# Ten instead of nine slots for the expert weights, in loops over five items

## What is computed

```
logits = xt @ w_router + b_router            # 256 x 32
top_vals, top_idx = top_k(logits, 4); gates = softmax(top_vals)
for each expert e, for its tokens xb:
    hgu  = xb @ w_up_gate[e] + b_up_gate[e]  # 1024 -> 2048
    glu  = minimum(hgu[:, :1024], 7); lin = clip(hgu[:, 1024:], -7, 7)
    hact = glu * sigmoid(1.702 * glu) * (lin + 1)
    y    = hact @ w_down[e] + b_down[e]      # 1024 -> 1024
    out[tokens] += gate * y
```

## Time and profile before

| | |
|---|---|
| time, median of 3 runs | 1927.2 us (1921.48 to 1930.23) |
| profiled execution, span from first to last instruction | 1927.9 us |
| TensorE busy | 1778.7 us (92%) |
| VectorE, ScalarE, GpSimd busy | 765.1, 494.2, 195.9 us |
| moved by the DMA queues | 554.21 MB, mean 287 GB/s |
| expert stage, from SyncE's first issue to TensorE's first work of the next stage | 167.8 to 1106.2 us |
| mean granted clock of TensorE | 0.979 of full speed |

### The profile page before, as it was taken

The page is one execution under the profiler, slowest core; times in us unless marked ns, Lnnn a source line. Parts: engine busy times, 40 slices in busy tenths (PEclk is TensorE's granted clock), DMA queues, the critical chain, the costliest instruction groups (busy, mean ns, idle before and its releaser), DMA issues. The chain is left out here.

```text
span 1927.9 us, 28825 instructions
## 1 busy us (share of the span) xinstructions
PE 1778.7 (92%) x11622; PEld 1109.2 (58%) x11622; DVE 765.1 (40%) x1324; ACT 494.2 (26%) x792; POOL 195.9 (10%) x141
## 2 busy tenths in 40 slices
PE   7998999999998998999988889999999999999997
PEld 6764333333333333333333368978998778858996
DVE  8844211111111011011111186946554764456554
ACT  4623100000000000000000145444442333224442
POOL 4620000000000000000000055430000104200000
PEclk8998999999999999999999999999999999999999
DMA  7365999999999999999999946564531532145530
GB/s 284 137 245 226 398 430 429 429 430 429 430 430 430 430 430 430 430 429 430 430 429 430 381 153 234 186 228 177 200 146 24 200 109 89 64 157 196 201 127 33
DMA packets 104725, 554.21 MB, mean 287 GB/s; under 512 B 17441, under 2 KB 27682, under 8 KB 79218
## 3 DMA queue, kind: packets, MB, share of 16 engines
q1 hardware_dynamic: 104370, 553.25, 70.7%
q10 hardware_dynamic: 288, 0.02, 0.0%
HBM read 551.15 MB, written 2.10 MB: 287 GB/s over the span
## 5 line engine op out<-in xcount | busy, mean ns | idle before, releaser
L1227 PE MATMUL banks<-front,xsT 128*64 128x512 f32 x1360 | 304.8, 599 | 19.8 <-DMA front<-in_w_up 19.1
L1408 DVE TENSOR_SCALAR xT<-banks 128x512 f32<-128x512 f32 x32 | 22.1, 692 | 638.4 <-PE banks L1234 638.4
L1227 PEld LDWEIGHTS banks<-front,xsT 128*64 128x64 f32 x1360 | 95.8, 138 | 222.4 <-issue 180.5
L1265 PE MATMUL banks<-front,hT 128*64 128x512 f32 x704 | 157.6, 600 | 15.1 <-ACT hT L1324 15.1
L1227 PE MATMUL banks<-more_slots,xsT 128*64 128x512 f32 x688 | 152.6, 594 | 8.7 <-DMA more_slots<-in_w_up 8.7
L2185 PE MATMUL banks<-f_xT_hi,f_w_hi 128*128 128x256 f32 x512 | 144.9, 283 | 1.5 <-DVE f_xT_lo L309 1.5
L2185 PE MATMUL banks<-f_xT_lo,f_w_hi 128*128 128x256 f32 x512 | 144.9, 283 | 0.0
L2185 PE MATMUL banks<-f_xT_hi,f_w_lo 128*128 128x256 f32 x512 | 144.9, 283 | 0.0
L1320 ACT ACTIVATE xT<-xT 128x512 f32<-128x512 f32 x32 | 20.1, 629 | 478.9 <-DVE xT L1408 478.9
L1227 PEld LDWEIGHTS banks<-more_slots,xsT 128*64 128x64 f32 x688 | 48.4, 137 | 110.4 <-issue 91.9
L1265 PEld LDWEIGHTS banks<-front,hT 128*64 128x64 f32 x704 | 49.0, 138 | 108.6 <-issue 89.2
(11 more groups left out here) (433 smaller groups left out, 2953.6 us busy)
## 6 DMA issues: line engine op xcount, KB each, us to landing
front<-in_w_up SPq DMA_DIRECT2D x85, 2048.0 KB, 34.9
front<-in_w_down SPq DMA_DIRECT2D x44, 2048.0 KB, 38.1
more_slots<-in_w_up SPq DMA_DIRECT2D x43, 2048.0 KB, 34.8
f_ring<-in_ffn_w SPq DMA_DIRECT2D x30, 2048.0 KB, 8.0
more_slots<-in_w_down SPq DMA_DIRECT2D x20, 2048.0 KB, 38.2
g_ring<-in_sgu_in SPq DMA_DIRECT2D x7, 2048.0 KB, 7.7
m_raw<-in_w_in SPq DMA_DIRECT2D x6, 2048.0 KB, 8.2
g_ring<-in_sgu_out SPq DMA_DIRECT2D x4, 2048.0 KB, 7.7
```

The source lines that it names most:

```text
L1227: ins = nc.tensor.matmul(c.banks[CAP * h:CAP * (h + 1), bank, :], xsT[:, k, :], up[:, o:o + BANK], start=k == 0, stop=False)
L1265: ins = nc.tensor.matmul(c.banks[CAP * h:CAP * (h + 1), DOWN, :], hT[:, at:at + CAP], down[:, o:o + BANK], start=k == 0, stop=k == KC - 1)
L1408: v.tensor_scalar(glu[:, :], c.banks[:, GLU, :], LIMIT, None, ALU.min).then_inc(glu_ready, 1)
```

## The change

`RING` becomes 10, so `more_slots` has four slots and `rest` lies in the fourth of them. Ten slots and six loads an item repeat after 30 loads, so the loops run over five items (`GROUP`), with three laps of the ring in a pass (`LAPS`). SyncE writes out items 1 to 5 and has five passes of five items; TensorE has six. The second loop begins with item 31 as before. The area for dynamic DMAs shrinks from 16,384 to 1,024 bytes a partition. All buffers that are opened before `more_slots`, and those of other stages, lie 15,360 bytes lower, and the expert stage's small buffers, opened after it, 1,024 bytes higher. The stage's highest address goes from 227,968 at most to 227,232 in the program.

```
-RING = FRONT + 3
+RING = FRONT + 4
+GROUP = 5
+LAPS = GROUP * FRONT // RING
...
-                return n * (3 * m) + (one * m + a)
+                return n * (GROUP * m) + (one * m + a)
...
                 def item(n, one):
                     for s in range(FRONT):
-                        if not isinstance(n, int) or one > 1 or s > 2:
+                        if not isinstance(n, int) or FRONT * one + s >= RING:
                             ago, last = divmod(s - RING, FRONT)
                             if last < UPS:
-                                sp.wait_ge(up_used, n * (3 * UPS) + ((one + ago) * UPS + last + 1))
+                                sp.wait_ge(up_used, n * (GROUP * UPS) + ((one + ago) * UPS + last + 1))
                             else:
...
-                        elif s == 2:
+                        elif FRONT * one + s == RING - 1:
                             sp.wait_ge(third_part, TC)
-                        load(n * 3 + one, s, (FRONT * one + s) % RING)
+                        load(n * GROUP + one, s, (FRONT * one + s) % RING)
...
-                for one in (1, 2, 3):
+                for one in range(1, GROUP + 1):
                     item(0, one)
-                with sp.Fori(1, (E - 2) // 3) as n:
-                    for one in (1, 2, 3):
+                with sp.Fori(1, (E - 2) // GROUP) as n:
+                    for one in range(1, GROUP + 1):
                         item(n, one)
...
-                        pe.wait_ge(landed[at], i[0] * 32 + 16 * (lap + 1))
+                        pe.wait_ge(landed[at], i[0] * (16 * LAPS) + 16 * (lap + 1))
...
-                with pe.Fori(0, (E - 2) // 3) as n:
-                    for one in (1, 2, 3):
+                with pe.Fori(0, (E - 2) // GROUP) as n:
+                    for one in range(1, GROUP + 1):
                         item((n, one), False)
...
-    nc = bacc.Bacc("TRN2", target_bir_lowering=False, num_devices=1)
+    nc = bacc.Bacc("TRN2", target_bir_lowering=False, num_devices=1, dynamic_dma_scratch_size=1024)
```

More of the change, by code:

```diff
@@ L1105, in item @@
                     for s in range(FRONT):
-                        if not isinstance(n, int) or one > 1 or s > 2:
+                        if not isinstance(n, int) or FRONT * one + s >= RING:
                             ago, last = divmod(s - RING, FRONT)
                             if last < UPS:
-                                sp.wait_ge(up_used, n * (3 * UPS) + ((one + ago) * UPS + last + 1))
+                                sp.wait_ge(up_used, n * (GROUP * UPS) + ((one + ago) * UPS + last + 1))
                             else:
-                                sp.wait_ge(down_used, n * (3 * DOWNS) + ((one + ago) * DOWNS + last + 1 - UPS))
-                        elif s == 2:
+                                sp.wait_ge(down_used, n * (GROUP * DOWNS) + ((one + ago) * DOWNS + last + 1 - UPS))
+                        elif FRONT * one + s == RING - 1:
                             sp.wait_ge(third_part, TC)
-                        load(n * 3 + one, s, (FRONT * one + s) % RING)
+                        load(n * GROUP + one, s, (FRONT * one + s) % RING)
                 def late_item(i, e):
@@ L1210, in weights @@
                     else:
-                        pe.wait_ge(landed[at], i * 16 + 16 * (lap + 1 + 2 * ((E - 2) // 3) - (E - 1)))
+                        pe.wait_ge(landed[at], i * 16 + 16 * (lap + 1 + LAPS * ((E - 2) // GROUP) - (E - 1)))
                     return slots[at]
```

## The result

| | before | after |
|---|---|---|
| median | 1926.24 us (1921.48 to 1930.23, 4 runs) | 1942.39 us (1937.23 to 1944.50, 4 runs) |
| ratio after / before | | 1.0065, 95% interval 1.0045 to 1.0084 |
| profiled execution, span | 1927.9 us | 1935.5 us |
| last sums of the expert stage (TensorE) | 1099.55 us | 1111.09 us |
| 16 KB blocks in the instruction queue of TensorE (q8) | 48 | 96 |

The quotient of the two medians is 1.0084; the ratio on record, which the text goes by, is lower. The forecast was 1922.3 us in a range of 1916 to 1930. The change was slower, by the second rival. In the profile the expert stage ends 11.5 us later. What comes behind it took 817.7 us against 821.7, which this profiled run (the fastest of the four) gave back; I have no cause for that part, and the profiles of the experiments differ there by a few microseconds too.

What follows compares the result with a forecast made beforehand. The prediction took the full weight-load queues of the expert stage as the bound. Its terms, -4.9 us for the tenth slot and 0 for loops and addresses, took the median from 1927.2 to 1922.3 us, range 1916 to 1930.

Steps and rivals of the forecast that it cites:

- the second rival: TensorE's branch back: five-item body isn't kept, code fetched again each pass; 1924 to 1958 us, chance 0.09.
- What bounds the kernel: Expert stage: full load queues at 429 to 430 GB/s set its end, 4.88 us a load.
- part 1: Tenth slot: one more load before item 0 gives a slot back, the whole stream earlier; -4.9 us.
- the two early holes: Idle queues in 182 to 184 and 190 to 192 us: 2.0 + 2.9 = 4.9 us, filled by one load.
- The third hole: Idle queues at 212 to 215 us, nearly 3 us, expected to stay until item 0's first down slot returns.
- the waits after 560 us: TensorE's waits in the expert stage: 40.3 us on its weight port, 19.1 on its own, for `front` alone.
- Part 3: 1 KB for dynamic DMAs and moved addresses: no work changes; term 0.
- Part 2: Loops over five items: TensorE's body grows from four blocks to seven, assumed kept; term 0.
- Blocks between 300 and 1060 us: Sign in TensorE's instruction queue: blocks there would show the five-item body is fetched again and the forecast wrong.
- The issue-to-landing time: Sign for weight loads in the expert stage: 39 to 40 us instead of 34.9.

Runs made afterwards that it cites:

- two parts: Changed kernel (ten slots, five-item loops) with TensorE's loop gathering two of its three parts, so the body spans six blocks: 1924.87 us, ratio 0.9966.
- half loads: Changed kernel with each weight load of items 6 to 31 bringing only half of its slot: 1919.70 us, two runs.

## Why the prediction was wrong

**What bounds the kernel, and part 1: right.** The queues were full, the two early holes were the place of the gain, and their filling is worth one load: 4.6 us in a body that fits, 4.9 between the two written-out kernels, 4.88 forecast. The third hole shrank as well in most profiles with ten slots, because TensorE's clock rose after 10.2 us and not after 17.1, so item 0 ran 2.8 us faster. Four of the six profiles with ten slots have the 10.2 us and none of the five with nine, so whether the slot has a part in it stays open. It isn't needed for the gain: two profiles with ten slots had 17.1 us, and one of these, with two parts, was as fast by its median. One reading was off: the waits after 560 us were not for `front` alone, those for loads into `more_slots` add 18.4 us on the weight port and 8.7 on TensorE's own. It changes nothing in the sum.

**Part 3: right,** by the run with 1 KB alone.

**Part 2: the step that failed.** I wrote that seven blocks, "one of them fetched ahead makes eight", just fit, and took 0. The runs show 52 us of TensorE's time in its place, 17 us more than the loads cover, against the 4.9 us gained. Two things were wrong in it. Blocks are fetched two ahead, not one: three blocks follow each branch, the one branched to and two more. Seven and two are nine, and nine blocks are fetched in each pass. And I let a rule for the memory's size decide where no row showed more than four blocks kept. The Trainium skill, "Runtime: NRT & Kernel Launch", "Instruction fetch mechanics", gives TensorE's instruction memory as 2,048 instructions in blocks of 256, eight blocks; by that rule and two blocks ahead six is the most that a body can span, which agrees with the runs. The runs themselves show only that six are kept and seven aren't; the eight is the Trainium skill's. Its other sentence, that a branch out of a window of two pages forces a fetch, holds for the body of seven and isn't borne out for those of four and six.

**The rival's price: wrong in its mechanism.** Rival 2 had the place (the branch back, five times) but took the weight loads for what would suffer, up to 36 us of one engine, and called TensorE's own stall "covered by the 10 us that it waits in five items". It was the stall: 7.8 us idle and some 2.5 of slower work behind it, 52 us in the stage (1110.4 - 1058). What covers it isn't a rate but a sum: up to the end that the loads allow. That was 38 us with nine slots (1061 to 1099), and is 35 with ten (214.34 + 843.8 = 1058 to 1093). 52 against 35 puts the stage's end 17 us behind what the loads would have allowed, and 11.5 behind before. The loads' own loss by code fetches was 0.11 us a block, a tenth of what I feared.

**The chances.** I gave this rival 0.09 on the ground that four blocks were kept "without a fault". That says nothing of seven; with a number of the Trainium skill that fits to the last block, and an unknown in it, an even chance would have been fairer, and the range should have reached to its price.

**The signs named ahead.** Blocks between 300 and 1060 us were named as what would prove rival 2, and there are 46 of them. The issue-to-landing time was to rise to 39 to 40 us; it fell to 22.7, and is 40.2 over the same stretch in the kernel that fits (41.4 in the shorter one above).

## What to carry to other kernels

A loop's code is a buffer too: before unrolling it further, count its instructions (here 331 an item) in 16 KB blocks and keep a TensorE body to six; beyond that each pass refetched it here and lost some 10 us at the branch with the queues full, 7 to 8 of them idle. Cover for such stalls is the sum that the engine has in hand up to where the other bound ends, and a change that moves that bound earlier uses it up. Writing the loop out removes the stalls but still pays for each block beside full queues; of a slot's gain of 5 us nothing was left.

## What the runs showed of the hardware that I had not expected

TensorE keeps a loop body of up to six blocks of 16 KB and, once it spans seven, fetches all of it again in each pass: nine blocks a pass, 96 in the run against 50. In each of the five stalls of the changed kernel its granted clock fell from 2.4 to 1.2 GHz: the lower level reaches 4 to 5 us into the next item and costs 1.9 to 2.4 us there. And blocks at a branch follow each other by 6 us when four to five weight loads are queued, against 3.5 to 4 us with half loads, when the queues are 63% busy.
